# Late attention: probabilities transposed by VectorE in squares of 32 and exchanged by DMA through memory

## The chip, the cores and the metric

The kernel runs on one core of one Trainium2 chip. Its time is the time of one execution on the device, in microseconds (us), the median of several runs. Engines: TensorE (PE; its weight loads PEld), VectorE (DVE), ScalarE (ACT), GpSimd (POOL), SyncE (SP). DMA transfers are issued from the queues of SP and ACT and carried by 16 DMA engines.

## What is computed

Two transformer blocks over 256 tokens of width 1024, all in float32: a first block (convolution mixer, attention and long convolution, each with a mixture of experts) and a second one of two layers. The change lies in the mixer of the second block, cut here to what matters:

```python
for l in range(DEPTH):                                   # 2 layers
    x = x + 0.5 * swiglu(rms_norm_2(x, ffn1_norm[l]), ...)
    z = rms_norm_2(x, mix_norm[l]) @ w_in[l]
    qa, ka, va, qs, ks_, vs, zg = jnp.split(z, splits, axis=-1)
    o_na = neighbourhood_attention(qa, ka, va, na_rpb[l])      # 8 heads of 64: softmax(q k + bias) v
    o_sw = sliding_window_gqa(qs, ks_, vs, t5_bias, sw_sink[l])  # 8 heads, 2 key heads, a sink in the sum
    g = jax.nn.sigmoid(zg + b_gate[l]).reshape(B, S, N_BRANCHES, D)
    merged = g[:, :, 0] * (o_na @ w_branch_na[l]) + g[:, :, 1] * (o_sw @ w_branch_sw[l])
    x = x + merged @ w_out[l]
    x = x + 0.5 * swiglu(rms_norm_2(x, ffn2_norm[l]), ...)
```

For each head, p is the softmax over 256 keys for 256 queries (256 x 256 numbers); the product p v sums over keys, so p is needed with the keys on the partitions, while the softmax has the queries there.

## The kernel before

Each engine has a program of its own, written out in order, and waits for the others through semaphores. `sync_program` streams all weights through a ring in pieces of 1 or 2 MB, in the order of use (line 844). `tensor_program`, `scalar_program`, `vector_program` and `pool_program` each have the same stages.

The late attention is in `mixer_2` of the tensor program (from line 1774) and in `layer` of the others. It goes through eight pairs of heads, m = 0 to 7; pairs 0 to 3 are of the first kind (neighbourhood), 4 to 7 of the second (window, with a sink). With each pair one gate column (m) of `w_in` is worked off beside it, in a seven-product scheme whose weight differences POOL makes. PE's loop (from line 1903) does for pair m: `turned(m - 1)` (lines 1862 to 1870), eight transposes of 128x128, four for each head, in banks 2 and 3; `scores(m)` (line 1847) into banks 0 and 1; `values(m - 2)` (line 1872) into bank 6; `gates_first(m)` and `gates_rest(m)` into banks 4 and 5. After the loop come the last transposes and values, and `branch(p, n)` (line 1888), sixteen products each; `branch(p, 1)` needs the outputs of all eight pairs.

DVE (loop from line 3493) does `softmax(m)` (line 3449): scores plus bias with their least value, line 3459, then, when the exponentials are there, the reciprocal of the sum (3466, 3468) and the scaling (3471); then `gates(m)` (line 3473), five additions and products over banks 4 and 5. PE may overwrite these banks with `gates_first(m + 1)` when `gate_sums` of m is done.

ACT (loop from line 2473) does `turned(m - 1)` (line 2467), two copies of the transposed probabilities from banks 2 and 3 into `y.PT`, with the order of the queries in each half reversed; `values(m - 2)` (line 2471), a copy into `y.OUT2`; `softmax(m)` (2455, 2459), the exponentials with their sums; `gate_first(m)` (2440); `gates(m - 1)` (2446), the sigmoids. Exponentials and sigmoids each load their table anew.

The feed-forward of the same layers turns its hidden units in another way: DVE transposes squares of 32 (line 3277), ACT writes the result to memory (`spill`, line 2313) and reads it back in another order, in pieces of 128 bytes (`bring_back`, line 2322). The bias of the first kind is read by SP in pieces of 256 bytes, four DMAs in a row (line 823).

## Time and profile before

| what | value |
|---|---|
| time, median of 3 runs (lowest to highest) | 2544.48 us (2544.22 to 2552.77) |
| the profiled execution's own time, and its span | 2544.48 us, 2543.2 us |
| mean granted clock of PE | 0.998 of full speed |
| PE busy | 2451.7 us (96%) |
| DVE, ACT, POOL busy | 1249.2 us (49%), 437.9 us (17%), 178.7 us (7%) |
| attention of layer 0, of layer 1 (on PE) | about 1612 to 1691 us, 2206 to 2285 us |
| DMA queue of SP; of ACT | 92304 packets, 682.66 MB; 101180 packets, 28.35 MB |

The span reaches from the first to the last instruction. Busy time is the time in which an engine executes; register, semaphore and DMA-issuing instructions are not counted. In a timeline a row gives the start, the length and the engine, the line, the operation with its output and inputs, and how many instructions were merged; in brackets stands the idle time before it and what ended it. ACTq and SPq are the DMA issues of an engine's own queue; their length is the time that the trace gives the issue itself, not the transfer. The waits and the chain name what an engine waited for.

### The profile page before, as it was taken

Reading aid. Unit: us, or ns where it says so; the run is one execution under the profiler, and the core shown is the slowest. Engines: PE = TensorE matmul, PEld = TensorE weight load, DVE = VectorE, ACT = ScalarE, POOL = GpSimd, SP = SyncE. Lnnn points to the kernel's source line nnn. Section 1 sums busy time; section 2 is a strip of 40 time slices with the busy share of each in tenths; the row PEclk is TensorE's granted clock in tenths of the full one; section 3 lists DMA queues with packets and bytes.
Section 4 is the critical chain, followed back from the end, with each engine's and each line's share of the span. In section 5 each row is a group of like instructions: output and inputs, shape, how many; then the busy total and the mean of one; then the engine's idle time right before and its main releaser. Section 6 shows DMA issues by size and latency. Waiting matters only on the chain.

```text
span 2543.2 us, 29763 instructions
## 1 busy us (share of the span) xinstructions
PE 2451.7 (96%) x12358; PEld 1567.5 (62%) x12358; DVE 1249.2 (49%) x2237; ACT 437.9 (17%) x1102; POOL 178.7 (7%) x126
## 2 busy tenths in 40 slices
PE   9999999888999999987889999999999999999999
PEld 5347443424578753332348866888866875888884
DVE  4994321212176621110117666545776775654774
ACT  2111110101123210000001002641101100470110
POOL 0011000000000000000000011430001003240000
PEclk9999999999999999999999999999999999999999
DMA  9854999999984499999999863415674974423671
GB/s 395 330 233 178 371 425 426 427 428 427 423 340 166 172 376 427 426 428 428 427 422 347 255 227 149 150 67 211 212 230 153 253 231 153 173 105 138 220 223 40
DMA packets 193618, 712.90 MB, mean 280 GB/s; under 512 B 117252, under 2 KB 121860, under 8 KB 128332
## 3 DMA queue, kind: packets, MB, share of 16 engines
q1 hardware_dynamic: 92304, 682.66, 67.6%
q10 hardware_dynamic: 101180, 28.35, 5.4%
q8 instruction: 98, 1.61, 0.3%
q14 instruction: 36, 0.29, 0.0%
HBM read 698.36 MB, written 12.60 MB: 280 GB/s over the span
## 4 chain that ended last, share of the span: by engine, by line
PE 79%; DMA 16%; DVE 4%; ACT 1%; issue 0%; POOL 0%; SPq 0%; another core or an unknown queue 0%; DVEq 0%; POOLq 0%
PE bank L867 77%; DMA ring<-in_stream 8%; DMA ring_high<-in_stream 4%; DMA ring_low<-in_stream 4%; PE bank L870 2%; DVE hidden L2892 1%; DVE ab_z L2717 1%; DMA hidden_turned<-normed 1%; DVE moe_results L2917 0%; POOL ab_ln_sum L3584 0%; DVE ring L3228 0%; DVE cd_y L2524 0%; DVE moe_turned L2913 0%; ACT normed L2243 0%; ACT hidden L2243 0%
## 5 line engine op out<-in xcount | busy, mean ns | idle before, releaser
L867 PE MATMUL bank<-ring,gates 128*128 128x256 f32 (+1 forms) x1760 | 433.6, 391 | 3.1 <-DVE ring L3228 2.1
L867 PE MATMUL bank<-ring,moe_chosen 128*64 128x512 f32 (+1 forms) x2352 | 400.3, 491 | 27.7 <-DMA ring<-in_stream 27.6
L867 PEld LDWEIGHTS bank<-ring,gates 128*128 128x128 f32 x1760 | 333.6, 190 | 70.7 <-issue 22.7
L867 PE MATMUL bank<-ring,normed 128*128 128x256 f32 x1448 | 339.6, 380 | 2.0 <-ACT normed L2328 1.3
L867 PEld LDWEIGHTS bank<-ring,moe_chosen 128*64 128x64 f32 x2352 | 150.6, 137 | 246.9 <-issue 200.4
L867 PEld LDWEIGHTS bank<-ring,normed 128*128 128x128 f32 x1448 | 273.1, 190 | 41.6 <-issue 3.9
L867 PE MATMUL bank<-normed,ring 128*128 128x256 f32 (+2 forms) x1152 | 289.8, 406 | 2.3 <-DVE normed L2698 1.5
L867 PEld LDWEIGHTS bank<-normed,ring 128*128 128x128 f32 x1152 | 189.4, 190 | 99.9 <-issue 85.4
L867 PE MATMUL bank<-ring,ffn_hidden 128*128 128x512 f32 (+1 forms) x416 | 179.3, 561 | 0.0
L2917 DVE COPY moe_results<-bank 32x512 f32<-32x512 f32 x36 | 24.8, 690 | 245.2 <-PE bank L867 244.8
L2908 DVE TENSOR_TENSOR moe_silu<-bank,moe_silu 128x512 f32<-128x512 f32 x32 | 22.1, 691 | 246.8 <-PE bank L867 246.8
L3228 DVE TENSOR_TENSOR ring<-ring,ring 128x1024 f32<-128x1024 f32 x117 | 142.1, 1215 | 1.6
L867 PE MATMUL bank<-ring,moe_turned 128*64 128x512 f32 x560 | 125.2, 595 | 17.4 <-DMA ring<-in_stream 14.3
L867 PEld LDWEIGHTS bank<-ring,ffn_hidden 128*128 128x128 f32 (+1 forms) x416 | 70.8, 182 | 86.3 <-issue 76.2
L2350 ACT ACTIVATE gates<-gates,small 128x256 f32<-128x256 f32 x88 | 44.4, 507 | 412.7 <-DVE gates L3241 226.2
L2164 ACT COPY moe_results<-bank 32x512 f32<-32x512 f32 x36 | 20.7, 575 | 467.1 <-PE bank L867 466.8
L867 PEld LDWEIGHTS bank<-ring,moe_turned 128*64 128x64 f32 x560 | 40.0, 137 | 98.6 <-issue 81.7
L2717 DVE SCALAR_TENSOR_TENSOR ab_z<-ab_pad_b,vectors,ab_z 128x512 f32<-128x512 f32 x120 | 90.2, 752 | 4.3
L3228 DVE TENSOR_TENSOR ring<-ring 128x1024 f32<-128x1024 f32 x71 | 85.8, 1208 | 0.0
L867 PE MATMUL bank<-ring,hidden 128*128 128x512 f32 x168 | 84.5, 592 | 0.0
L3308 DVE TENSOR_TENSOR ring<-ring 128x512 f32<-128x512 f32 x88 | 62.1, 705 | 38.2 <-PE bank L867 38.2
L3600 POOL TENSOR_TENSOR na_bias<-na_bias,na_mask 128x512 f32<-128x512 f32 x16 | 21.4, 1370 | 782.5 <-PE bank L867 782.5
(468 smaller groups left out, 2705.4 us busy)
## 6 DMA issues: line engine op xcount, KB each, us to landing
ring<-in_stream SPq DMA_DIRECT2D x318, 1024.0 KB, 7.3
ring<-in_stream SPq DMA_DIRECT2D x117, 2048.0 KB, 30.8
ring_low<-in_stream SPq DMA_DIRECT2D x7, 2048.0 KB, 43.8
ring_far<-in_stream SPq DMA_DIRECT2D x7, 2048.0 KB, 44.6
ring_high<-in_stream SPq DMA_DIRECT2D x6, 2048.0 KB, 44.8
hidden_turned<-normed ACTq DMA_DIRECT2D x44, 256.0 KB, 7.2
ffn_hidden<-hidden_turned ACTq DMA_DIRECT2D x44, 256.0 KB, 7.4
hidden<-in_stream SPq DMA_DIRECT2D x9, 1024.0 KB, 30.9
```

The costliest lines, as they stand in the source:

```text
L867: return nc.tensor.matmul(o, lhsT, rhs, start=start, stop=stop, skip_group_check=True)
L870: return nc.tensor.transpose(o, x, ident[0:x.shape[0], 0:x.shape[0]])
L2164: ins = nc.scalar.copy(m.YG[CAP * e:CAP * e + CAP, i, 0:512], bank[4][CAP * i:CAP * i + CAP, :])
L2350: nc.scalar.activation(y.sg[:, t, :], (y.C2 if t else y.C1)[:, 0, :], ACT.Silu, scale=y.rinv_t[:, t:t + 1]).then_inc(*done.up((tag, l, "si ...
L2717: ins = v.scalar_tensor_tensor(out=z_j, in0=ab.PB[:, :, k:k + T], scalar=tap("conv_b", k, j), in1=z_j, op0=ALU.mult, op1=ALU.add)
L2892: v.scalar_tensor_tensor(out=H[:, s, n, :], in0=bank[5 + n % 3][:, T * i:T * i + T], scalar=M.MOD[:, l, 5, n, s:s + 1], in1=H[:, s, n, :], ...
L2908: v.tensor_tensor(m.SG, bank[1][:, :], m.SG, ALU.mult).then_inc(*done.up((tag, "hidden", g, e)))
L2917: ins = v.tensor_copy(m.YG[CAP * e:CAP * e + CAP, i, 512:1024], bank[4][64 + CAP * i:64 + CAP * i + CAP, :])
L3228: v.tensor_tensor(tw[:, i], a, b, ALU.subtract).then_inc(*done.up((tag, l, "t", c, i)))
L3308: v.tensor_tensor(to[:, i], a, b, ALU.subtract).then_inc(*done.up((tag, l, "dt", c, i)))
L3600: nc.gpsimd.tensor_tensor(part, part, mask, ALU.add).then_inc(*done.up(("na_bias", l, t) if h == NA_H - 2 else None))
```

## The change

For pairs 0 to 6 the transposes on PE and the copies on ACT go. The probabilities of a pair lie in one tensor `y.SC` of 128x1024, ordered so that squares of 32x32 follow each other (`probs_of`; pair 7 keeps the plain order). DVE transposes all squares at once into `y.turned`. ACT writes that to memory with four DMAs (`spill_probs`, 32 partitions each, rows of 512 bytes), and one pair later reads it back with two DMAs in pieces of 128 bytes (`bring_probs`) into `y.pairs`, which holds the keys on the partitions. The values of a pair are computed three pairs later (`LAG`) in place of two, from there; pair 7 is still transposed by PE and copied by ACT. The reversal of the queries is now in ACT's copy of the values. DVE's order changes: a gate column's sums and scaling are split into `gates_first`, `gates_summed` and `gates_scaled`, the latter two placed in the next pair around `biased`. Behind the loop, PE does values(5), two branches, values(6), values(7), then the other branches; values(7) has bank 7.

The diff, without the new semaphores and the two buffers in memory:

```diff
--- before.py
+++ after.py
@@ -614,9 +614,9 @@
     y.keys_by_token = y.C1[:, :, 0:P]
     y.sq8, y.sq8_heads = M.H[:, 1], heads[:, 0:KB * T].rearrange("p (n t) -> p n t", t=T)
     y.hid, y.hid_turned = spare[:, 0:512], ctx_u[:, 0:512]
-    y.SC = [spare[:, 512 * n:512 * n + 512].rearrange("p (t k) -> p t k", t=TT) for n in range(2)]
-    y.PT = [[x[:, 512 * n:512 * n + 512].rearrange("p (k q) -> p k q", k=TT) for n in range(2)]
-            for x in (spare[:, 1024:2048], M.ring[WEIGHT_SUMS[0]][:, SLOT:SLOT + 1024])]
+    y.SC, y.turned = spare[:, 0:1024], spare[:, 1024:2048]
+    y.pairs = [M.ring[WEIGHT_SUMS[0]][:, SLOT + 1024 * n:SLOT + 1024 * n + 1024] for n in range(2)]
+    y.PT = [[x.rearrange("p (k i q) -> p i k q", k=TT, i=2)[:, i] for i in range(2)] for x in y.pairs]
     y.t1 = [y.KA[:, 2 * n:2 * n + 2, :] for n in range(2)]
     y.g8, y.stats = [M.small[:, 2 * l:2 * l + 2] for l in range(LAYERS)], M.small[:, 16:16 + 16 * 8]
     y.rinv_t, y.rinv_8 = M.small[:, 144:144 + TT], M.small[:, 146:146 + TT]
@@ -696,6 +696,16 @@
 def wide(x, n):
 
     return x.rearrange("p (o t) -> p o t", o=1).broadcast_to([P, n, x.shape[1]])
+
+
+def probs_of(y, m, i, t):
+
+    order = "i t k f" if m == NA_H - 1 else "k i t f"
+    return y.SC.rearrange(f"p ({order}) -> p i t k f", i=2, t=TT, f=32)[:, i, t]
+
+
+def by_pieces(x):
+    return x.rearrange("p (k f) -> p k f", f=32)
 
 
 def reversed_queries(x):
@@ -853,6 +865,8 @@
 
 
 VALUES_BANK = (4, 5)
+VALUES_AT = (6,) * (NA_H - 1) + (7,)
+LAG = 3
 KEYS_BANK = 6
 
 
@@ -1862,11 +1876,9 @@
         def turned(m):
             for i in range(2):
                 pe.wait_ge(*V.at(("probs_2", l, m, i)))
-                if m:
-                    pe.wait_ge(*A.at(("turned_2", l, m - 1, i)))
                 for k in range(TT):
                     for t in range(TT):
-                        ins = turn(bank[2 + i][:, T * k + P * t:T * k + P * t + P], y.SC[i][:, t, P * k:P * k + P])
+                        ins = turn(bank[2 + i][:, T * k + P * t:T * k + P * t + P], flat(probs_of(y, m, i, t)[:, 4 * k:4 * k + 4]))
                 ins.then_inc(*done.up(("turned_2", l, m, i)))
 
         def values(m):
@@ -1877,12 +1889,11 @@
                 pe.wait_ge(*V.at(("head_normed", l, "ks")))
             if kind:
                 pe.wait_ge(*V.at(("vs", l)))
-            for i in range(2):
-                pe.wait_ge(*A.at(("turned_2", l, m, i)))
+            pe.wait_ge(*(A.at(("turned_2", l, m, 1)) if m == NA_H - 1 else S.probs_in.at((l, m))))
             for k in range(TT):
                 for i, (h, p0) in enumerate(heads):
                     v = y.VS[:, k, DH * (h // 4):DH * (h // 4) + DH] if kind else y.VA[:, k, DH * h:DH * h + DH]
-                    ins = mm(bank[6][p0:p0 + DH, 0:T], v, y.PT[m % 2][i][:, k, :], k == 0, k == TT - 1)
+                    ins = mm(bank[VALUES_AT[m]][p0:p0 + DH, 0:T], v, y.PT[m % 2][i][:, k, :], k == 0, k == TT - 1)
             ins.then_inc(*done.up(("values_2", l, m)))
 
         def branch(p, n):
@@ -1893,6 +1904,8 @@
             pe.wait_ge(*A.at(("out_2", l, NA_H // 2 * (n + 1) - 1)))
             if p >= 2:
                 pe.wait_ge(*V.at(("gated", l, p - 2, n)))
+            elif p:
+                pe.wait_ge(*A.at(("turned_2", l, NA_H - 1, n)))
             for half in range(2):
                 for k in range(4):
                     ins = mm(bank[b][:, T * half:T * half + T], ring.tile(name)[:, k, 256 * off + P * half:256 * off + P * half + P],
@@ -1902,20 +1915,19 @@
 
         pairs = NA_H
         for m in range(pairs):
-            if m:
-                turned(m - 1)
             scores(m)
-            if m >= 2:
-                values(m - 2)
+            if m >= LAG:
+                values(m - LAG)
             gates_first(m)
             gates_rest(m)
             if m == 1:
                 keys_turned()
         turned(pairs - 1)
+        values(pairs - 3)
+        branch(0, 0)
+        branch(1, 0)
         values(pairs - 2)
-        branch(0, 0)
         values(pairs - 1)
-        branch(1, 0)
         branch(0, 1)
         branch(1, 1)
         for p in range(2, KB // 2):
@@ -2456,34 +2468,57 @@
                                          bias=M.sinks[:, l, h:h + 1]).then_inc(*done.up())
                 for t in range(TT):
                     n = 2 * i + t
-                    nc.scalar.activation(y.SC[i][:, t, :], y.SC[i][:, t, :], ACT.Exp, bias=st[:, n:n + 1], scale=-1.0,
+                    nc.scalar.activation(probs_of(y, m, i, t), probs_of(y, m, i, t), ACT.Exp, bias=st[:, n:n + 1], scale=-1.0,
                                          accum_out=st[:, 4 + n:5 + n]).then_inc(*done.up(("exp_2", l, m, i, t)))
+
+        def spill_probs(m):
+
+            act.wait_ge(*V.at(("turned_2", l, m)))
+            if m >= 2:
+                act.wait_ge(*S.probs_in.at((l, m - 2)))
+            for a in range(4):
+                rows = bass.AP(tensor=probs_blocks[m % 2].tensor, offset=a * 32 * 1024, ap=[[128, 32], [32 * 128, 8], [1, 128]])
+                nc.scalar.dma_start(rows, y.turned[32 * a:32 * a + 32, :].rearrange("p (k n) -> p k n", k=8)).then_inc(
+                    *S.probs_out.up((l, m) if a == 3 else None))
+
+        def bring_probs(m):
+
+            act.wait_ge(*S.probs_out.at((l, m)))
+            if m >= 2:
+                act.wait_ge(*TE.at(("values_2", l, m - 2)))
+            for k in range(TT):
+                rows = probs_blocks[m % 2].rearrange("(a k p x f) -> k p x a f", a=4, k=TT, p=P, f=32)[k]
+                to = y.pairs[m % 2].rearrange("p (k x a f) -> p k x a f", k=TT, a=4, f=32)[:, k]
+                nc.scalar.dma_start(to, rows).then_inc(*S.probs_in.up((l, m) if k == TT - 1 else None))
 
         def turned(m):
             for i in range(2):
                 act.wait_ge(*TE.at(("turned_2", l, m, i)))
-                if m >= 2:
-                    act.wait_ge(*TE.at(("values_2", l, m - 2)))
-                nc.scalar.copy(reversed_queries(flat(y.PT[m % 2][i])), bank[2 + i][:, :].rearrange("p (n q) -> p n q", q=P)).then_inc(*done.up(("turned_2", l, m, i)))
+                act.wait_ge(*TE.at(("values_2", l, m - 2)))
+                nc.scalar.copy(y.PT[m % 2][i], bank[2 + i][:, :].rearrange("p (k q) -> p k q", k=TT)).then_inc(*done.up(("turned_2", l, m, i)))
 
         def values(m):
             act.wait_ge(*TE.at(("values_2", l, m)))
-            nc.scalar.copy(y.OUT2[:, m, :], bank[6][:, 0:T]).then_inc(*done.up(("out_2", l, m)))
+            nc.scalar.copy(reversed_queries(y.OUT2[:, m, :]), bank[VALUES_AT[m]][:, 0:T].rearrange("p (n q) -> p n q", q=P)).then_inc(*done.up(("out_2", l, m)))
 
         for m in range(NA_H):
             if m:
-                turned(m - 1)
+                spill_probs(m - 1)
             if m >= 2:
-                values(m - 2)
+                bring_probs(m - 2)
             softmax(m)
+            if m >= LAG:
+                values(m - LAG)
             gate_first(m)
             if m:
                 gates(m - 1)
             if m == 1:
                 keys_out()
+        values(NA_H - 3)
         turned(NA_H - 1)
+        bring_probs(NA_H - 2)
+        gates(NA_H - 1)
         values(NA_H - 2)
-        gates(NA_H - 1)
         values(NA_H - 1)
         squares("ffn2", y.sq8_heads, lambda p: V.at(("hidden", l, "mix", p)))
         ffn(2)
@@ -2496,6 +2531,7 @@
 
     distances = nc.dram_tensor("distance_bias", (SW_H, 2 * T), F32, kind="Internal").ap()
     turned_blocks = [nc.dram_tensor(f"hidden_turned{i}", (P * 2 * T,), F32, kind="Internal").ap() for i in range(2)]
+    probs_blocks = [nc.dram_tensor(f"probs_turned{i}", (P * 4 * T,), F32, kind="Internal").ap() for i in range(2)]
     mixer_ab()
     moe(0, "ab")
     mixer_cd()
@@ -3446,19 +3482,22 @@
             v.tensor_copy(y.KSX[0:DH, :], y.KS[DH:P, :]).then_inc(*done.up())
             v.tensor_copy(y.KSX[DH:P, :], y.KS[0:DH, :]).then_inc(*done.up(("ks_swapped", l)))
 
-        def softmax(m):
+        def biased(m):
             kind, blk = divmod(m, NA_H // 2)
             st = y.stats[:, 64 * (m % 2):64 * (m % 2) + 64]
             dve.wait_ge(*TE.at(("scores_2", l, m)))
             dve.wait_ge(*(I["sw_bias"].at(TT - 1) if kind else S.pool.at(("na_bias", l, TT - 1))))
             for i in range(2):
                 h, top = 2 * blk + i, st[:, 2 * i:2 * i + 2]
-                if m:
-                    dve.wait_ge(*TE.at(("turned_2", l, m - 1, i)))
                 for t in range(TT):
-                    v.tensor_tensor_reduce(out=y.SC[i][:, t, :], in0=bank[i][:, T * t:T * t + T], in1=(y.SW_BIAS if kind else y.NA_BIAS)[:, h, t, :],
+                    v.tensor_tensor_reduce(out=probs_of(y, m, i, t), in0=by_pieces(bank[i][:, T * t:T * t + T]),
+                                           in1=by_pieces((y.SW_BIAS if kind else y.NA_BIAS)[:, h, t, :]),
                                            scale=-1.0, scalar=y.minus_sinks[:, h:h + 1] if kind else -3.0 * NEG, op0=ALU.add, op1=ALU.min,
                                            accum_out=top[:, t:t + 1]).then_inc(*done.up(("biased", l, m, i) if t else None))
+
+        def probs(m):
+            kind = m // (NA_H // 2)
+            st = y.stats[:, 64 * (m % 2):64 * (m % 2) + 64]
             for i in range(2):
                 total, extra = st[:, 4 + 2 * i:6 + 2 * i], st[:, 8 + 2 * i:10 + 2 * i]
                 dve.wait_ge(*A.at(("exp_2", l, m, i, TT - 1)))
@@ -3468,22 +3507,36 @@
                 v.reciprocal(total, total).then_inc(*done.up())
                 dve.wait_ge(*done.now())
                 for t in range(TT):
-                    v.tensor_scalar(y.SC[i][:, t, :], y.SC[i][:, t, :], total[:, t:t + 1], None, ALU.mult).then_inc(*done.up(("probs_2", l, m, i) if t else None))
-
-        def gates(c):
-
+                    part = probs_of(y, m, i, t)
+                    v.tensor_scalar(part, part, total[:, t:t + 1], None, ALU.mult).then_inc(*done.up(("probs_2", l, m, i) if t else None))
+
+        def turned(m):
+            dve.wait_ge(*done.at(("probs_2", l, m, 1)))
+            if m:
+                dve.wait_ge(*S.probs_out.at((l, m - 1)))
+            v.transpose(y.turned, y.SC).then_inc(*done.up(("turned_2", l, m)))
+
+        def gate_parts(c):
             b, d = (bank[x][:, :].rearrange("p (n t) -> p n t", t=P) for x in VALUES_BANK)
-            to = y.gates_of[c].rearrange("p (n t) -> p n t", t=P)
+            return b, d, y.gates_of[c].rearrange("p (n t) -> p n t", t=P)
+
+        def gates_first(c):
+            b, d, to = gate_parts(c)
             dve.wait_ge(*A.at(("gate_first", l, c)))
-            v.tensor_tensor(to[:, 0:4:3, :], b[:, 1:3, :], wide(to[:, 3, :], 2), ALU.add).then_inc(*done.up())
+            v.tensor_tensor(to[:, 0:4:3, :], b[:, 1:3, :], wide(to[:, 3, :], 2), ALU.add).then_inc(*done.up(("gate_firsts", l, c)))
+
+        def gates_summed(c):
+            b, d, to = gate_parts(c)
             dve.wait_ge(*S.chunk.at(("in_2", l, 9 + c)))
-            dve.wait_ge(*done.now())
+            dve.wait_ge(*done.at(("gate_firsts", l, c)))
             v.tensor_tensor(to[:, 1:3, :], d[:, 0:2, :], wide(to[:, 3, :], 2), ALU.add).then_inc(*done.up())
             dve.wait_ge(*done.now())
             v.tensor_tensor(to[:, 3, :], to[:, 1, :], d[:, 1, :], ALU.add).then_inc(*done.up())
             dve.wait_ge(*done.now())
             v.tensor_tensor(to[:, 1:3, :], to[:, 1:3, :], d[:, 2:4, :], ALU.add).then_inc(*done.up(("gate_sums", l, c)))
-            dve.wait_ge(*done.now())
+
+        def gates_scaled(c):
+            dve.wait_ge(*done.at(("gate_sums", l, c)))
             by_block = y.gates_of[c].rearrange("p (n t) -> p n t", t=T)
             v.tensor_tensor(by_block, by_block, wide(y.rinv, 2), ALU.mult).then_inc(*done.up(("gate", l, c)))
 
@@ -3491,12 +3544,21 @@
         dve.wait_ge(*done.now())
         dve.wait_ge(*S.chunk.at(("in_2", l, 8)))
         for m in range(NA_H):
-            softmax(m)
+            if m:
+                gates_summed(m - 1)
+            biased(m)
+            if m:
+                gates_scaled(m - 1)
+            probs(m)
+            if m < NA_H - 1:
+                turned(m)
+            gates_first(m)
             if m == 0:
                 keys_scaled()
             if m == 2:
                 keys_swapped()
-            gates(m)
+        gates_summed(NA_H - 1)
+        gates_scaled(NA_H - 1)
         dve.wait_ge(*A.at(("gate", l, KB - 1)))
         for p in range(KB // 2):
             for n in range(2):
```

## Rows read from the trace of the kernel before

**Rows 1.** Stretches: length, busy PE, PEld, DVE, ACT, POOL, clock, DMA share, GB/s.

```profile
1652.00:1662.00 10.00, 10.00 (x88) 8.92 (x87) 5.75 (x21) 8.12 (x21) 5.94 (x5) 1.00 0.31 107
...
2246.00:2256.00 10.00, 10.00 (x88) 8.93 (x87) 5.75 (x21) 8.12 (x21) 5.80 (x5) 1.00 0.33 107
```

**Rows 2.** Chain of waits, 1600 to 1700 us, shares by line.

```profile
by line: PE bank L867 92.1%; PE bank L870 8.1%
```

**Rows 3.** Timeline of PE, one pair: start, us, line, operation, tiles, shape.

```profile
1656.47 1.04 PE L870 MATMUL bank<-kept,hidden 128*128 128x128 f32 x8
...
1657.43 1.13 PE L867 MATMUL bank<-ffn_hidden 64*128 64x256 f32 x8
...
1658.50 1.08 PE L867 MATMUL bank<-ring,ffn_hidden 128*64 128x256 f32 x8
...
1659.51 2.05 PE L867 MATMUL bank<-normed,ring 128*128 128x128 f32 x16
...
1664.97 1.06 PE L867 MATMUL bank<-normed,ring 128*128 128x128 f32 x8
...
1665.87 1.04 PE L870 MATMUL bank<-kept,hidden 128*128 128x128 f32 x8
```

**Rows 4.** One line's instructions, DVE's transpose: ns min/median/max, first and last start.

```profile
L3277 DVE STREAM_TRANSPOSE normed<-hidden x44: 711/711/712, 1366.2 to 2473.1; 128x512 f32<-128x512 f32 x44
```

**Rows 5.** Timeline of DVE, the same pair, after the last exponential.

```profile
1663.79 0.16 DVE L3466 TENSOR_TENSOR small<-small 128x2 f32<-128x2 f32 x1 [0.16 <-ACT hidden L2459]
...
1664.19 0.61 DVE L3471 TENSOR_SCALAR hidden<-hidden,small 128x256 f32<-128x256 f32 x2
```

**Rows 6.** Timeline of ACT, the same pair.

```profile
1660.02 1.28 ACT L2455 ACT_TABLE_LOAD   x1
...
1663.67 0.24 ACT L2440 COPY gates<-bank 128x128 f32<-128x128 f32 x1
...
1666.50 1.08 ACT L2467 COPY ring<-bank 128x512 f32<-128x512 f32 x2 [0.37 <-PE bank L870]
```

**Rows 7.** DMA issues of three lines: ns of the issue, min/median/max.

```profile
L2313 ACTq DMA_DIRECT2D hidden_turned<-normed x44: 326/4628/16291, 1366.9 to 2473.9; - x44
...
L2322 ACTq DMA_DIRECT2D ffn_hidden<-hidden_turned x44: 587/587/4127, 1374.3 to 2485.2; - x44
...
L823 SPq DMA_DIRECT2D na_bias<-in_na_rpb x32: 601/636/1218, 1372.3 to 2009.0; - x32
```

**Rows 8.** Timeline of ACT (ACTq: its DMA issues), two places in the feed-forward.

```profile
1455.27 0.59 ACTq L2322 DMA_DIRECT2D ffn_hidden<-hidden_turned  x1
...
1457.08 0.60 ACTq L2313 DMA_DIRECT2D hidden_turned<-normed  x1
...
1770.54 0.37 ACT L2328 COPY normed<-bank 128x256 f32<-128x256 f32 x1 [0.49 <-PE bank L867]
...
1770.54 0.61 ACTq L2322 DMA_DIRECT2D ffn_hidden<-hidden_turned  x1
...
1771.40 4.71 ACTq L2313 DMA_DIRECT2D hidden_turned<-normed  x1
...
1776.64 0.51 ACT L2350 ACTIVATE gates<-gates,small 128x256 f32<-128x256 f32 x1 [5.74 <-DVE gates L3241]
```

**Rows 9.** DMA: one load's landing, 1656 to 1664; queues, 1770.5 to 1774 (packets, MB, share).

```profile
ring<-in_stream SPq DMA_DIRECT2D x1, 1024.0 KB, 4.9
...
q1 hardware_dynamic: 179, 1.34, 96.1%
```

**Rows 10.** Timeline of ACT and PE, end of the last pair.

```profile
1682.38 0.19 ACT L2459 ACTIVATION_READ_ACCUMULATOR hidden<-hidden,small 128x1 f32 x1
...
1685.63 1.08 PE L867 MATMUL bank<-hidden,ffn_hidden 128*64 128x256 f32 x8
...
1686.65 3.72 PE L867 MATMUL bank<-normed,ring 128*128 128x256 f32 x16
...
1686.76 0.37 ACT L2471 COPY normed<-bank 128x256 f32<-128x256 f32 x1 [0.39 <-PE bank L867]
```

More of the change, by code:

```diff
@@ L725, in signals @@
     S.hidden = Signal(nc, "in_hidden", known, 16)
+    S.probs_out = Signal(nc, "out_probs", known, 16)
+    S.probs_in = Signal(nc, "in_probs", known, 16)
     S.sent = Signal(nc, "out_sent", known, 16)
@@ L3613, in program @@
     pool_program(nc, a, M, S, ring)
-    every = [S.tensor, S.scalar, S.vector, S.pool, S.chunk, S.distance, S.spilled, S.hidden, S.sent, *S.landed, *S.into.values()]
+    every = [S.tensor, S.scalar, S.vector, S.pool, S.chunk, S.distance, S.spilled, S.hidden, S.probs_out, S.probs_in, S.sent, *S.landed, *S.into.values()]
     return {x.name: x.table for x in every}
```

## The prediction

> **What bounds the kernel now.** I read three views in this order. The table by stretches shows the stage that changes: in ten microseconds of late attention TensorE (PE) is busy for all ten at full clock, ScalarE (ACT) for 8.12, VectorE (DVE) for 5.75, and the DMA engines for a third of the time; layer 1 looks the same [rows 1]. The chain of waits over layer 0's attention is PE alone, 8.1% of it transposes [rows 2]. So PE's work is the time here, and a microsecond taken from it is one gained, as long as ACT, DVE and the transfers keep up. PE's timeline gives the slots of one pair, from start to start: transposes 1656.47 to 1657.43, 0.96; scores 1.07; values 1.01; gates 5.46, then 0.90 more. The next transposes start at 1665.87, a period of 9.40 [rows 3].
>
> The profiled execution took 2544.48 us, of which the span is 2543.2; it is also the median of the three runs shown, so the sum is made against 2544.5.
>
> **Taken from PE.** Transposes of seven pairs in each of two layers leave: 14 x 0.96 = 13.4 us [rows 3]. That is the ceiling of the gain. The period could fall to 8.44. The reversed order of queries moves from one copy to another of the same kind: nothing.
>
> **Put on DVE.** One transpose of 128x1024 a pair. The trace has 128x512 at 0.71 [rows 4]; between that and twice it, 1.42, I take 1.3, since it has twice the elements. DVE was busy for 5.75 of 10 [rows 1], 5.4 a pair, and with 1.3 still has room under 8.44. What counts is its place: spill_probs waits for it. From the last exponential, DVE's row of sums starts at 1663.79 and the scaled rows end at 1664.80 [rows 5]; with the transpose and its hand-overs that is 2.4 us from exponential to first spill (2.2 for the first kind, which has no sink).
>
> **Put on ACT: six DMA issues a pair.** This decides. Two copies go (1.08 [rows 6]); four spills and two brings come, in ACT's own order. Behind them wait the exponentials of the next pair, behind those DVE's scaling and gates_first, and behind those PE's gates of the pair after. A DMA issue holds what follows on its queue: the spill of the feed-forward takes 0.33 at least, 4.63 in the median, 16.3 at most; its bring, of 128-byte pieces as here, 0.59 in the median [rows 7]. The timeline says why: a spill issued 0.25 after a bring took 4.71, one issued 1.2 after a bring in a quiet stretch 0.60 [rows 8]. The second issue is held while the first transfer's pieces are not yet drained. The change has two brings of 2048 pieces each, one right behind the other, with four spills ahead of them.
>
> Call B the time from the first spill to the end of the second bring.
> - Low end: every issue at its lowest row, 4 x 0.33 + 2 x 0.59, with five gaps of 0.04: 2.7 us.
> - Issues back to back, nothing held: the loads of na_bias, four in a row on SP, have 0.64 each [rows 7]. 0.33 + 3 x 0.68 + 2 x 0.63 = 3.6 us.
> - High end: the second bring held as the feed-forward's spill is, from 1770.54 to 1776.11 = 5.6 [rows 8]: 0.33 + 3 x 0.68 + 5.6 = 8.0 us.
> - I take 4.8. With nothing else on the queues the spills' pieces should be gone some 3.5 us after the first issue, and then the second bring is taken: 4.1 (an estimate, from the 0.60 in the quiet stretch). On top, a weight load of 1 MB lands 4.9 us after its issue, and in the 3.5 us after the bring at 1770.54 only the weight queue moved, 179 packets and none of ACT's [rows 9]. One load falls into each pair, and I let it cost 0.7 on average. Between ends of 2.7 and 8.0 this lies nearest to the unheld case, because the attention's DMA share is a third, not full.
>
> The Trainium skill, page DMA: Bandwidth & Descriptors, section Queues, rings and completion order, says that each DMA engine takes turns between the queues; the 179 packets disagree. By its rule the 0.7 would be nothing and the sum 8 us lower.
>
> **The sum.** From one pair's last exponential to the next: 2.4 to the transpose's end, B, then 3.75 from ACT's table load at 1660.02 to the end of the last exponential, 0.1 after the copy's start at 1663.67 [rows 6]. So 6.15 + B for the second kind, 5.55 + B for the first. ACT's other work (values, gate copy, table load and sigmoids) lies beside DVE's 2.4, and a DMA can be issued while a copy still runs (bring and copy begin together at 1770.54 [rows 8]). With B = 4.8 a pair takes 10.95 or 10.35 in place of 9.40: ACT sets the pace, not PE. Spills run from pair 1, brings from pair 2:
> - pair 1: one lot of spills ahead of its exponentials, partly beside DVE's work: +0.5
> - pairs 2 and 3: 2 x 0.95 = +1.9
> - pairs 4 to 7: 4 x 1.55 = +6.2
> - end: before, the last exponential ended at 1682.57 and the last transposes' slot at 1685.63 [rows 10], 3.06 later, since PE was at the gates. A PE that waits has done those and needs 1.6: -1.5
> - new order behind it: values(7) stands right ahead of branch(0, 1), which needs ACT's copy of it; before, a branch of 3.7 us lay between. Copy 0.37 and two hand-overs: +0.65. values(6) waits for the last two brings, which ACT issues after its copies of the last pair; two branches, 7.4 us, cover them: nothing. Without that cover it would be what is left of a bring's landing, up to those 7.4 [rows 10].
>
> That is 7.8 a layer, 15.6 in both: 2544.5 + 15.6 = **2560 us**. One microsecond of B is 12 us of the time (six pairs, two layers). Values three pairs behind hide the landings: a bring has the rest of its pair, some 5 us, and the values behind it another; PE has slack of two microseconds by then.
>
> **Rivals.**
> - Issues aren't held. B is 2.7 to 3.6; then the first kind's pair takes 8.44 to 9.15 and the second's 8.85 to 9.75, and the time is 2536 to 2546: not slower. One mechanism, deciding from B = 3.3, where the second kind's period is again 9.40. For it: the one quiet row, 0.60. Against it: 2048 pieces stood alone ahead of that one. The Trainium skill, same page, section Issuing engines are not separate DMA queues, calls the time to initiate a DMA usually small beside the DMA; by that this rival would be the likely one, and the 4.71 of the rows speaks against it.
> - The second bring is held as the feed-forward's spill is, in each pair: B = 8.0, 54 us more, 2598. For it: the median of 4.63. Against it: where those issues are held, weights pass without a break, 1.34 MB in 3.5 us [rows 9]; the attention has 1 MB in a whole pair.
> - ACT's DMA issues run wholly beside its arithmetic, and PE stays the bound: 13.4 less twice 0.65, 2532. Against it: the activation after the 4.71 us issue began only when that was over (1776.64 [rows 8]).
>
> **How the numbers follow.** Forecast, 2552 to 2571: 0.50. Issues not held, 2536 to 2551: 0.25. Held throughout, 2572 to 2600: 0.20. PE the bound, 2532: 0.05. The range 2536 to 2590 leaves out the last and the upper half of the third. About 0.5% (12.7 us) is what a measurement of this kernel can tell from no change. Faster by more needs nearly the whole ceiling: 0.03. Slower by more, above 2557: all of the held case and three quarters of the forecast, 0.57. The rest, 0.40, is within.
>
> **What would show it.** In the profile after: ACT's DMA rows of the second bring near 1.5 us and up; the pair's period on PE near 10.9 in the second half, with idle time of PE that ends on DVE's gate sums; and no PE work for seven of eight transposes. A period of 8.4 and PE at ten in ten would show me wrong, and so would a second bring at 0.6.

## The result, and the profile after

The changed kernel takes 2588.24 us (median of six runs, 2587.23 to 2589.01) against 2544.26 for the kernel before beside it: 1.0168 times, with an interval of 1.0155 to 1.0182. The forecast was 2560, with a range of 2536 to 2590: slower, as forecast, and inside the range, but by 44 us in place of 16.

The page after: PE is busy for 95% of a longer span, though it has less to do; ACT's DMA queue carries 14.7 MB more.

```profile
span 2587.7 us, 29613 instructions
...
PE 2456.8 (95%) x12246; PEld 1571.3 (61%) x12246; DVE 1280.6 (49%) x2251; ACT 421.5 (16%) x1074; POOL 179.1 (7%) x126
...
q10 hardware_dynamic: 174204, 43.03, 8.2%
```

The table by stretches over the attention of layer 0 (length; busy PE, PEld, DVE, ACT, POOL; granted clock; DMA share; GB/s) answers [rows 1]. PE was busy for ten of ten there. Now it has gaps in every stretch, and from the second on its granted clock is a mean of 0.80 to 0.87, so for part of the time the lower of its two levels (1.2 and 2.4 GHz), which also makes its busy time longer.

```profile
1613.80:1641.00 27.20, 23.99 (x203) 21.91 (x202) 16.00 (x53) 12.22 (x37) 13.50 (x11) 1.00 0.63 181
1641.00:1667.00 26.00, 20.99 (x146) 18.38 (x147) 17.23 (x47) 13.91 (x38) 8.84 (x7) 0.80 0.68 157
1667.00:1692.00 25.00, 19.39 (x146) 17.23 (x144) 15.44 (x41) 11.15 (x27) 9.74 (x8) 0.86 0.69 170
1692.00:1718.00 26.00, 20.98 (x128) 17.41 (x129) 11.40 (x36) 12.96 (x33) 0.44 (x1) 0.87 0.56 140
```

One pair on ACT's timeline, from the last exponential of pair 3 to that of pair 4 (start, us, line; L2471 exponentials, L2481 spills, L2492 brings, L2467 the sink's exponential):

```profile
1653.13 0.18 ACT L2471 ACTIVATION_READ_ACCUMULATOR hidden<-hidden,small 128x1 f32 x1
...
1655.47 1.34 ACTq L2481 DMA_DIRECT2D probs_turned<-hidden  x3
...
1656.85 0.50 ACTq L2481 DMA_DIRECT2D probs_turned<-hidden  x1
1657.38 5.32 ACTq L2492 DMA_DIRECT2D ring<-probs_turned  x2
1662.73 1.28 ACT L2467 ACT_TABLE_LOAD   x1 [5.46 <-issue]
...
1666.29 0.19 ACT L2471 ACTIVATION_READ_ACCUMULATOR hidden<-hidden,small 128x1 f32 x1
```

The three parts of the forecast's sum can be read off. From 1653.31, the end of the exponentials, 2.16 to the first spill; B, from 1655.47 to the end of the second bring at 1662.70, is 7.23; 3.78 more to the end of the next exponentials. Between bring and exponentials ACT does nothing: 5.46 us of idle time, put down to its own issues. Together 13.2, where before a pair took 9.40 [rows 3]. All pairs of the two layers, read in the same way (the parts of a pair add up to its time):

| us | pair 2 | 3 | 4 | 5 | 6 | 7 |
|---|---|---|---|---|---|---|
| layer 0: exponentials to first spill | 4.09 | 3.43 | 2.16 | 5.08 | 2.36 | 2.36 |
| B | 8.23 | 4.22 | 7.23 | 4.68 | 6.88 | 3.96 |
| end of bring to end of exponentials | 3.40 | 3.40 | 3.78 | 3.77 | 3.77 | 3.77 |
| layer 1: exponentials to first spill | 4.18 | 4.60 | 2.16 | 5.94 | 2.36 | 2.36 |
| B | 7.23 | 3.88 | 7.52 | 3.85 | 6.95 | 4.36 |

ACT's waits over layer 0's attention (1612 to 1722 us: total, times, longest) point the same way. They put the idle time ahead of the exponentials down to the landing of ACT's own spills or to its issues; the exponentials themselves wait for no landing, and the rows above show the issues back to back, with gaps of 0.04 at most, so that the length of the issues is what holds them.

```profile
ACT L2467 <- DMA probs_turned<-hidden: 17.5, 3, 7.2
...
ACT L2471 <- DMA probs_turned<-hidden: 7.8, 1, 7.8
ACT L2467 <- issue: 5.5, 1, 5.5
```

From pair 0 to pair 7 the exponentials now take 84.2 us in layer 0 and 84.9 in layer 1, against 65.2 before: 38.6 us of the 44.5 by which the span grew. The ends of the two layers, from pair 7's exponentials to `branch(0, 1)`, account for 2.5 and 1.4 more, and 1.6 lie ahead of the attention, in stages that the change doesn't touch. (Layer 0's first scores start at 1612.24 before and 1613.82 after; over the ten profiled executions of this document they start between 1609.92 and 1613.82.)

### The profile page after: what moved, and what is told of

The parts are those of the page before. It is cut to its first block, busy times and chain, and to the rows that moved or that the text cites. A ratio compares the mean times of both kernels' runs of the same rounds, so it can differ in the third digit from the quotient of the medians.

```text
span 2587.7 us, 29613 instructions
## 1 busy us (share of the span) xinstructions
PE 2456.8 (95%) x12246; PEld 1571.3 (61%) x12246; DVE 1280.6 (49%) x2251; ACT 421.5 (16%) x1074; POOL 179.1 (7%) x126
## 4 chain that ended last, share of the span: by engine, by line
PE 74%; DMA 16%; DVE 5%; ACT 2%; ACTq 1%; issue 1%; POOL 0%; another core or an unknown queue 0%; DVEq 0%; POOLq 0%
PE bank L881 73%; DMA ring<-in_stream 7%; DMA ring_high<-in_stream 4%; DMA ring_low<-in_stream 4%; PE bank L884 2%; ACTq L2492 1%; DVE hidden L2928 1%; DVE ab_z L2753 1%; DMA hidden_turned<-normed 1%; ACT hidden L2471 1%; DMA probs_turned<-hidden 1%; DVE hidden L3511 0%; DVE hidden L3517 0%; ACT L2467 0%; ACTq L2481 0%
## 5 line engine op out<-in xcount | busy, mean ns | idle before, releaser
L881 PE MATMUL bank<-normed,ring 128*128 128x256 f32 (+2 forms) x1152 | 301.3, 420 | 31.1 <-DVE gates L3536 16.9
L881 PEld LDWEIGHTS bank<-normed,ring 128*128 128x128 f32 x1152 | 199.6, 202 | 130.5 <-issue 116.4
L881 PE MATMUL bank<-ring,ffn_hidden 128*128 128x512 f32 (+1 forms) x480 | 188.9, 543 | 9.6 <-ACT ring L2458 5.3
```

Source lines behind the costliest of these rows:

```text
L881: return nc.tensor.matmul(o, lhsT, rhs, start=start, stop=stop, skip_group_check=True)
```

## The experiments

The theory from the trace: the six DMA issues on ACT's queue stand in front of the exponentials and set the pace (B), and PE waits. Rivals: VectorE's new order, or the longer way through memory itself, is what costs. What B consists of is a second question, and what else made the loss so large a third. Each kernel ran beside the kernel before, which had 2544.3 (first four) and 2544.6 (last four) there.

**The issues moved from ACT to SP**, to the place where SP waits for pair m's gate column to come free; the same DMAs, ahead of that column's load; each bring also waits until the one before has landed.

```diff
         for m in range(NA_H):
-            if m:
-                spill_probs(m - 1)
-            if m >= 2:
-                bring_probs(m - 2)
             softmax(m)
...
         for i, n in transfers(ring.plan):
+            if ring.to_be_free(i, n) in after_chunk:
+                l, m = after_chunk[ring.to_be_free(i, n)]
+                if m < NA_H - 1:
+                    spill_probs(l, m)
+                if m:
+                    bring_probs(l, m - 1)
             if ring.to_be_free(i, n):
                 sp.wait_ge(S.chunk.sem, ring.to_be_free(i, n))
```

> The changed kernel with its spills and brings issued by SP, at the point where SP would wait for the pair's gate column to be free, and with each bring waiting for the landing of the one before it. Theory H (ACT is held by its DMA issues, 5.8 us a pair from the first spill to the end of the second bring, and that sets the pair's period): ACT's list falls to 6.5 us, PE's slots of 8.44 set the pace again in most pairs, 2532 to 2548 us. Rival O (the new order of DVE's work, DVE's longer list and the values three pairs behind cost the time, the issues little): 2575 to 2590 us. Rival P (transfers land too late for the values, wherever they are issued): idle time of PE ahead of the values, 2560 or more.

Measured: 2544.62 (2542.34 to 2550.44), 1.0004 times before (0.9995 to 1.0014). All of the 44 us are gone while the same bytes go the same way through memory, and VectorE has the same work and order. In the late pairs PE is without a gap and its period is 8.53, the 8.44 of the forecast's ceiling within 0.1. On PE's timeline (no row has an idle time before it), scores, values, and gates follow each other at 1657.77 and 1666.30:

```profile
1657.77 1.13 PE L916 MATMUL bank<-ffn_hidden 64*128 64x256 f32 x8
1658.83 1.08 PE L916 MATMUL bank<-ring,ffn_hidden 128*64 128x256 f32 x8
1659.85 2.05 PE L916 MATMUL bank<-normed,ring 128*128 128x128 f32 x16
1661.74 3.74 PE L916 MATMUL bank<-gates,ring 128*128 128x128 f32 x32
1665.31 1.06 PE L916 MATMUL bank<-normed,ring 128*128 128x128 f32 x8
1666.30 1.14 PE L916 MATMUL bank<-ffn_hidden 64*128 64x256 f32 x8
```

So the place of the issues is the cause. But nothing of the 13.4 us was gained: PE's waits in the attention of layer 0 (below) were 3.6 us for VectorE's gate sums, in pairs 1 and 3, and 1.0 for ACT's copies of values in the end. The granted clock was 0.92 from 1634 to 1655: behind the second of those waits 48 matmuls of the gates took 3.41 and 4.02 in place of 2.05 and 3.74, 1.6 more.

```profile
PE bank L916 <- DVE ring L3545: 3.6, 2, 2.2
PE bank L916 <- ACT normed L2517: 1.0, 2, 0.6
```

**The brings in pieces of 2048 bytes**, 128 to a DMA in place of 2048 of 128 bytes, which puts what `values` reads in another order.

```diff
-                rows = probs_blocks[m % 2].rearrange("(a k p x f) -> k p x a f", a=4, k=TT, p=P, f=32)[k]
-                to = y.pairs[m % 2].rearrange("p (k x a f) -> p k x a f", k=TT, a=4, f=32)[:, k]
+                rows = probs_blocks[m % 2].rearrange("(p k n) -> k p n", k=TT, p=P)[k]
+                to = y.pairs[m % 2].rearrange("p (k n) -> p k n", k=TT)[:, k]
```

> The changed kernel with brings that read as many bytes in pieces of 2048 bytes (128 in each DMA in place of 2048); the probabilities come in the wrong order, so the attention's values are not those of the reference. Theory H, with the hold set by the number of pieces not yet drained: the second bring is issued in about 0.6 us, first spill to end of second bring 3 to 3.6 us in every pair in place of 4 to 8, about 2.4 us less in each of twelve pairs: 2553 to 2563 us. Were the hold set by bytes, or by the weight loads alone: 2580 to 2590. Rival O: 2585 to 2590.

Measured: 2553.68 (2552.64 to 2561.70), 1.0042 times before (1.0028 to 1.0057). B is 3.72 in the mean of the twelve pairs, a little above the 3 to 3.6 that were expected. The brings' issues (ns, min/median/max), in the changed kernel and then in this one:

```profile
L2492 ACTq DMA_DIRECT2D ring<-probs_turned x28: 587/968/5203, 1633.0 to 2323.4; - x28
```

```profile
L2492 ACTq DMA_DIRECT2D ring<-probs_turned x28: 326/530/1591, 1632.3 to 2288.7; - x28
```

The hold on the second bring is that of the many small pieces: with the same bytes in few pieces it is all but gone. Even so the kernel is slower than before, since the four spills and two brings still stand in the pair's chain.

**The second bring behind the exponentials.**

```diff
                 spill_probs(m - 1)
             if m >= 2:
-                bring_probs(m - 2)
+                bring_probs(m - 2, (0,))
             softmax(m)
+            if m >= 2:
+                bring_probs(m - 2, (1,))
```

> The changed kernel with ACT's second bring moved behind the exponentials, some 4 us after the first. Theory H: the second bring finds the first drained and takes 0.6, so that 2.5 us lie ahead of the exponentials and 0.6 behind: a pair of about 9.1 to 9.8 us, 2545 to 2560 us in all. Rival O: 2585 to 2590 us.

Measured: 2553.95 (2551.66 to 2556.72), 1.0039 times before (1.0025 to 1.0054). 34 us come back by moving one issue of six. Part of the hold remains, now in front of the gate's copy: in pair 2 the second bring takes 4.23 us, the exponentials that were already on the engine run beside it, and the copy waits for 2.21.

```profile
1634.44 4.23 ACTq L2492 DMA_DIRECT2D ring<-probs_turned  x1
...
1636.31 0.19 ACT L2471 ACTIVATION_READ_ACCUMULATOR hidden<-hidden,small 128x1 f32 x1
1638.71 0.27 ACT L2452 COPY ring<-bank 128x128 f32<-128x128 f32 x1 [2.21 <-issue]
```

**VectorE's new order alone**, in the kernel before (PE's transposes and ACT's copies kept, no exchange).

```diff
         for m in range(NA_H):
-            softmax(m)
+            if m:
+                gates_summed(m - 1)
+            biased(m)
+            if m:
+                gates_scaled(m - 1)
+            probs(m)
+            gates_first(m)
...
-            gates(m)
```

> The kernel before with only DVE's new order (a gate column's sums and scaling placed around the next pair's bias), transposes on PE and values two pairs behind as they were. Theory H: PE stays the bound, the same time as before within 3 us, 2541 to 2548. Rival O: a part of the loss shows here, 2555 us or more.

Measured: 2544.90 (2542.17 to 2546.66), 1.0001 times before (0.9991 to 1.0010). The new order costs nothing by itself, so this rival falls.

**Small weight loads during the attention.**

```diff
+            if ring.to_be_free(i, n) in late_chunks:
+                to, src = to[:, 0:128], src[:, 0:128]
             nc.sync.dma_start(to, src).then_inc(*ring.arrival(i).up(i if last else None))
```

> The changed kernel with the weight loads that SP issues as the gate columns of late attention come free (8 a layer) cut to 64 KB of their 1 MB; what they should have brought are weights of later stages, so the output is not the reference's. B, from ScalarE's first spill to the end of its second bring, is 8.2, 4.2, 7.2, 4.7, 6.9, 4.0 in pairs 2 to 7 of layer 0 of the changed kernel. Theory: the long ones have a load's packets ahead of ScalarE's on the engines. Without them B is 4.0 to 4.5 in every pair, 12 x 1.4 = 17 us less: 2571 (2565 to 2575). Rival 1 (the second bring is held by its own queue's pieces alone, and alternates with something of the attention's own order): B keeps its two values, 2588 within 3. Rival 2 (all of the hold is the loads'): B falls to 3.0 to 3.6, 2558 to 2563.

Measured: 2564.26 (2562.30 to 2566.71), 1.0080 times before (1.0065 to 1.0095) and 24.0 below the changed kernel. B is 4.82, 4.25, 4.99, 3.94, 3.85, 5.51 in layer 0 and 3.84 to 4.52 in layer 1: 4.33 in the mean, in place of 5.75. The brings' issues here:

```profile
L2500 ACTq DMA_DIRECT2D ring<-probs_turned x28: 587/954/2980, 1629.1 to 2297.8; - x28
```

So B is about 4.3 by itself, and 1.4 on average, some 3 in every second pair, is the weight load that SP has just issued; both rivals fall. The trace of the changed kernel shows the load at work. In layer 0 the loads are issued at 1630.4, 1657.5 and 1682.1, within 2 us of the first spills of pairs 2, 4 and 6, and at 1638.3, 1666.0 and 1690.6, by the end of these pairs' brings or behind it; none is issued during B in pairs 3, 5 and 7. From 1659.5 to 1661.5, while pair 4's second bring is held, the weight queue moved 92 packets (0.75 MB) and ACT's queue 4; pairs 2 and 6 have such a stretch too (80 packets against 1 from 1632.2 to 1634.2, 94 against none from 1683.8 to 1686.2). The time fell by 7 us more than 12 x 1.42 = 17: see the price of B below.

**GpSimd's weight differences left out.**

```diff
-                nc.gpsimd.tensor_tensor(gt[:, i], *terms[i], ALU.subtract).then_inc(*done.up(("gate_t", l, c, i)))
...
-            gate_product(d[:, P:2 * P], y.GT[c % 2][:, 0], y.US[:, 0])
+            gate_product(d[:, P:2 * P], tile[:, 0:4, P:2 * P], y.US[:, 0])
```

> The changed kernel (2588.2 us) without GpSimd's weight differences in late attention: the gate products of PE take the raw weight tile in the place of the differences, so the gates are not those of the reference; PE's count of matmuls is the same. In the trace of the changed kernel, VectorE takes 2.2 to 2.4 us from the last exponential to the end of its transpose, but 3.4 after pair 2 and 5.1 after pair 4 of layer 0, where GpSimd works on its differences in the same microseconds (scaling of two blocks 2.14 and 2.51 us in place of 0.61). Theory: GpSimd's work slows VectorE's on the path. Then these two stretches fall to 2.2 to 2.4, 1.1 + 2.7 us a layer, and the time to about 2580 (2577 to 2583). Rival: VectorE is slowed by the transfers that read its tile, or by the banks: then the two stretches stay long, and the time is 2588 within 2.

Measured: 2575.77 (2573.76 to 2578.74), 1.0124 times before (1.0111 to 1.0138) and 12.5 below the changed kernel, somewhat more than expected. B is unchanged, 5.70 in the mean. The stretches from the exponentials to the first spill that were 3.43 and 5.08 in layer 0, 4.60 and 5.94 in layer 1, are 2.16, 2.35, 2.16 and 2.36: 19.05 has become 9.03, 10.0 us. That of pair 2 is 4.09 in both layers. In the changed kernel, DVE's rows after pair 4's exponentials stand against GpSimd's (POOL) like this:

```profile
1666.10 1.38 POOL L3634 TENSOR_TENSOR ring<-ring 128x512 f32<-128x512 f32 x1 [3.01 <-PE bank L881]
1667.55 1.27 POOL L3634 TENSOR_TENSOR ring<-ring,ring 128x512 f32<-128x512 f32 x1
1668.78 1.31 POOL L3634 TENSOR_TENSOR ring<-ring 128x512 f32<-128x512 f32 x1
1670.05 1.31 POOL L3634 TENSOR_TENSOR ring<-ring,ring 128x512 f32<-128x512 f32 x1
```

```profile
1666.50 0.99 DVE L3505 TENSOR_TENSOR small<-small 128x2 f32<-128x2 f32 x1 [0.16 <-ACT hidden L2471]
...
1667.73 2.51 DVE L3511 TENSOR_SCALAR hidden<-hidden,small 128x256 f32<-128x256 f32 x2
1670.27 1.25 DVE L3517 STREAM_TRANSPOSE hidden<-hidden 128x1024 f32<-128x1024 f32 x1
```

and without GpSimd's work:

```profile
1664.03 0.62 DVE L3508 TENSOR_SCALAR hidden<-hidden,small 128x256 f32<-128x256 f32 x2
1664.68 1.25 DVE L3514 STREAM_TRANSPOSE hidden<-hidden 128x1024 f32<-128x1024 f32 x1
```

A sum of two numbers a partition takes 0.99 in place of the 0.16 of [rows 5] and ends at 1667.49, where GpSimd's first difference ends (1667.48); two scalings take 2.51 in place of 0.62. The transpose, which runs beside the last of the four, is not slowed. Nor are VectorE's rows that read a bank: the bias of pair 4 (line 3493) takes 0.48 for each 128x256 from 1658.58 to 1660.20, beside GpSimd's differences, and 0.48 from 1696.87, where GpSimd is idle; the gate's product behind it, between tiles, takes 1.77 in place of 0.69.

```profile
1658.58 0.48 DVE L3493 CUSTOM_DVE_ANT_0 hidden<-bank,sw_bias,small 128x256 f32<-128x256 f32 x1
...
1660.20 1.77 DVE L3541 TENSOR_TENSOR ring<-ring,late_rinv 128x512 f32<-128x512 f32 x1
```

**Eight transposes a pair back on PE, unread**, ahead of the scores of pairs 1 to 7.

```diff
+        def turned_unread():
+            for i in range(2):
+                for k in range(4):
+                    turn(bank[2 + i][:, P * k:P * k + P], U[:, 0, k, 0:P])
         for m in range(pairs):
+            if m:
+                turned_unread()
             scores(m)
```

> The changed kernel with the eight transposes a pair put back on PE ahead of the scores of pairs 1 to 7, on other data, into the free banks 2 and 3, and read by nobody: 14 x 0.96 = 13.4 us more of PE's work. Theory (ScalarE's queue sets the pace of the pair, PE waits): the 13.4 us fall into PE's waits, and the time stays at 2588 within 2; it falls to 2583 to 2586 if, with shorter idle time, PE's granted clock in the attention (0.80 to 0.87 in the changed kernel) comes back towards 1.0 and the last transposes end nearer to the last exponential than 3.6 us. Rival (PE is still the bound of most pairs): 2588 + 13 = 2601, or what part of it lies on the path.

Measured: 2580.85 (2578.94 to 2582.66), 1.0143 times before (1.0129 to 1.0157). With 13.4 us more of work for PE the kernel is 7.4 us faster than the changed one, more than the 2 to 5 us that were expected at best. The rival, that PE still bounds most pairs, falls. The granted clock over the attention (the same columns as above) is higher, and 1.00 in the end:

```profile
1638.00:1663.00 25.00, 18.88 (x144) 17.10 (x143) 16.50 (x44) 11.99 (x30) 9.03 (x7) 0.86 0.67 165
1663.00:1688.00 25.00, 21.83 (x174) 19.43 (x173) 16.33 (x45) 12.86 (x34) 10.05 (x8) 0.93 0.67 169
1688.00:1713.00 25.00, 21.50 (x144) 17.16 (x145) 10.58 (x33) 12.08 (x30) 2.10 (x1) 1.00 0.61 148
```

The last transposes now end 1.75 after pair 7's exponentials in both layers, where the changed kernel has 3.67 and 2.59. That is 2.8 of the 7.4; most of the rest is a shorter B in pair 6 (5.47 and 5.58 for 6.88 and 6.95).

**SP's issues, the keys' work moved, and another end.** From the first experiment's kernel (the waits that follow from PE's and ACT's new order change with it):

```diff
             biased(m)
             if m:
                 gates_scaled(m - 1)
+            if m == 1:
+                keys_scaled()
+            if m == 3:
+                keys_swapped()
             probs(m)
...
-            if m == 0:
-                keys_scaled()
-            if m == 2:
-                keys_swapped()
...
         branch(0, 0)
-        branch(1, 0)
-        values(pairs - 2)
         values(pairs - 1)
+        values(pairs - 2)
+        branch(1, 0)
         branch(0, 1)
```

> The kernel whose spills and brings SP issues (2544.6 us), with two more edits: VectorE works on the keys (their scaling and their swap) while ScalarE makes the exponentials of pairs 1 and 3, and not behind pairs 0 and 2; and behind the loop PE does values(5), branch(0,0), values(7), values(6), branch(1,0), branch(0,1), so that a branch covers each copy of values. Theory: the losses left there were PE's waits for VectorE's gate sums in pairs 1 and 3 (1.44 and 2.21 us, and 1.6 for the low clock after the second) and 1.03 in the end of a layer. Without them 2544.6 - 2 x 5.7 = 2533 (2531 to 2537), close to before less the 13.4 us of transposes. Rival: the waits move on (VectorE's gate sums stay late for another reason, or values(6) waits for its bring's landing): 2541 to 2545.

Measured: 2537.08 (2532.58 to 2538.68), 0.9969 times before (0.9956 to 0.9981): faster than the kernel before, by 7.5 us (0.3%, clear of 1 by its interval), and than the changed one. PE's waits over layer 0's attention are down to these (layer 1 has 1.0 for the gate sums and 1.7 for the brings):

```profile
PE bank L916 <- DVE ring L3546: 1.0, 2, 0.7
PE bank L916 <- DMA ring<-probs_turned: 0.7, 1, 0.7
```

From layer 0's first scores to the start of `branch(0, 1)` it is 78.5 us (1613.82 to 1692.28, the latter from the start of `branch(1, 0)` at 1688.63 and 3.65 for a branch), against 82.7 before (1612.24 to 1694.96): 4.3 of the 6.7 that a layer's transposes cost. The 2532 of the forecast's third rival, PE as the bound, is thus some 5 us away once another engine issues the DMAs and these waits of PE are shortened; the rival's mechanism, issues that run beside ACT's arithmetic, is not what got there. The time lies at the upper edge of what was expected; the waits above are part of what is left.

## Why the prediction came out as it did

**What bounds the kernel before, and the ceiling.** Right: with nothing in ACT's way the pair takes 8.53 on PE.

**The mechanism.** Right: ACT's issues stand ahead of the exponentials, ACT sets the pace, PE waits, and the time rises. Moving the issues takes away all of it, and PE's extra work fits into its waits. The signs that the forecast named are there: a second bring from 1.33 to 5.20 us, PE waiting for VectorE's gate sums, and a pair of 10.1 to 13.6 in the second half (forecast 10.95).

**The size: the step that failed.** The forecast's sum was 15.6, the difference measured 44. What failed is the price of three terms. VectorE's stretch from exponentials to spill was taken as undisturbed in every pair, with ACT's other work beside it at nothing and GpSimd's not thought of: 2 x (2 x 2.2 + 4 x 2.4) = 28.0 in the sum, 41.1 measured. A weight load was to cost B 0.7 on average: it cost 1.4. And the end of a layer was to be 0.85 shorter: it was 2.5 and 1.4 longer. The result lies in the stretch that the forecast gave 0.20 (held throughout, 2572 to 2600), not in its own (2552 to 2571, given 0.50), and the range held it only because it reached into that rival. Term by term:

- B, "I take 4.8": the mean is 5.75, 0.95 x 12 = 11.4 us. The 4.1 of the forecast without loads was near the 4.33 measured without them. What failed is the 0.7 for the weight load: it takes 1.4 on average, since in every second pair the load stands ahead of nearly the whole bring (B of 6.9 to 8.2, where the forecast's high end was 8.0) and in the others it doesn't (3.9 to 4.7). The forecast took the two ends for rival cases; they alternate.
- VectorE's 2.4 from exponential to spill: twelve stretches sum to 41.1 in place of 28.0, 13.1 us, more than B. Where nothing disturbs them they are 2.16 and 2.36, as forecast, and the transpose is 1.25 for 1.3. But in pairs 3 and 5 GpSimd works at the same time: 9.8 us of the 13.1. The trace before has this too (scalings of 0.35 in the median, the longest 1.355), beside a PE that was the bound, and the forecast didn't look for it. And for pair 2, "ACT's other work lies beside DVE's 2.4" was wrong: sigmoids and the keys' copy, which waits for PE, come ahead of the spill, 1.9 and 2.0 us; without GpSimd it is still 4.09 there.
- The end, -1.5 + 0.65: from pair 7's exponentials to `branch(0, 1)` 14.93 and 13.84 were measured, 12.40 before and 11.55 by the forecast, 5.7 us off in both layers. PE was to stand ready and need 1.6; it needed 3.6 in layer 0, because it had waited for the gate sums and then ran at a low clock. PE's timeline at this place, changed kernel, shows 16 matmuls of 3.76 behind that wait where [rows 3] have 2.05, and two waits of 0.47 and 0.56 for the copies of values. Only one of these had been counted, and the third values that a lag of three leaves behind the loop (1.0) not at all.

```profile
1697.10 3.76 PE L881 MATMUL bank<-normed,ring 128*128 128x128 f32 x16 [2.69 <-DVE gates L3536]
...
1705.74 1.04 PE L884 MATMUL bank<-kept,hidden 128*128 128x128 f32 x8
1706.71 1.08 PE L881 MATMUL bank<-ring,ffn_hidden 128*64 128x256 f32 x8
...
1716.38 1.08 PE L881 MATMUL bank<-ring,ffn_hidden 128*64 128x256 f32 x8 [0.47 <-ACT normed L2502]
1718.03 2.18 PE L881 MATMUL bank<-normed,ring 128*128 128x256 f32 x9 [0.56 <-ACT normed L2502]
```

- The other way go pairs 2 and 4, which took 10.49 and 9.77 before and not 9.40 (-2.9), and pair 1 (-0.5). 11.4 + 13.1 + 5.7 - 3.4 = 26.8; with 15.6 that is 42.4 of 44, and 1.6 lie ahead of the attention.

**The landings.** "Values three pairs behind hide the landings" failed once a layer. PE's row of values(0), in pair 3 of layer 0, has 5.34 us of idle time before it. The waits put it down to a sigmoid of ACT that ends at that moment, but `values` has no wait for a sigmoid; it waits for the second bring of pair 0, which was issued at about 1633.7 and landed after 10.9 us (the longest landing of that line), at 1644.6, as the row begins. In layer 1 the wait at this place is 1.08 and put down to the bring. The wait of layer 0 lies beside ACT's own chain, but the 16 matmuls behind it took 3.75 in place of 2.05.

```profile
1644.66 1.98 PE L881 MATMUL bank<-ring,ffn_hidden 128*64 128x256 f32 x8 [5.34 <-ACT ring L2458]
1647.98 3.75 PE L881 MATMUL bank<-normed,ring 128*128 128x128 f32 x16 [1.35 <-DVE ring L3536]
```

**The price of B.** "One microsecond of B is 12 us" was too low between these kernels: from 5.75 to 4.33 (small loads) the time fell by 24.0, from there to 3.72 (long pieces) by 10.6, 17 us for one. The profiled executions show what the rest is. Between those of the changed kernel and of the small loads, 25.7 us apart, B gives 17.0, VectorE's stretches from exponentials to spill 2.4, and the ends of the layers 2.8 (13.0 in both, from 14.93 and 13.84); 3.4 lie ahead of the first attention, where the edit changes nothing. From the small loads to the long pieces, 8.8 us apart, B gives 7.4 and VectorE's stretches 4.9, and the part ahead of the attention takes 2.8 back. So B itself costs its 12, and the rest is VectorE's stretches, the ends, and scatter ahead of the attention; why the stretches and the ends shrink with B no run separates.

**The rivals.** "Issues aren't held" fell: the median of 0.97 over all 28 brings hides that the first of each two takes 0.6 and the second up to 5.2. The Trainium skill, page DMA: Bandwidth & Descriptors, section Issuing engines are not separate DMA queues, calls the time to initiate a DMA usually small beside the DMA; here the second bring's was 1.3 to 5.2 against landings of 5.5 in the median, and the loss was gone when SP had the issues. "Held in each pair" came nearest in its number, 2598, but a B near its 8.0 comes in every second pair only; that the time came so near is in part luck, since VectorE's stretches and the ends make up much of it.

## What to carry to other kernels

Here a DMA issue cost its engine up to 5.2 us while the pieces ahead of it drained: put an exchange of many small pieces on a queue behind which no work of the path stands, and count the loads of other queues in the same stretch as part of its price. When a step moves onto another engine, look also at which engine beside it will then run in the same microseconds, and price the whole stretch with rows that ran beside that engine's work, not with the median. PE, which was the bound and now waits, got slower at its own work, too: 16 matmuls of 3.76 in place of 2.05.

## What the runs showed of the hardware

- Some of VectorE's instructions are held while GpSimd works, all of them between tiles in SBUF, the core's on-chip memory: 0.99 us for a sum of two numbers a partition (0.16 alone), ending with GpSimd's instruction within 0.01; 2.51 for two scalings (0.62 alone); 1.77 for the gate's product of 128x512 (0.69 in the pairs beside it). VectorE's transpose of squares, 1.25, and its bias rows, which read a bank (0.48 with and without), were not held beside GpSimd. The Trainium skill, page SBUF — State Buffer, section SBUF: two separate sides, describes an exclusive lock on a port pair that VectorE and GpSimd share, held for a whole instruction; these rows agree.
- A load of 1 MB passed nearly as a block: 92 of its packets and 4 of ACT's in the 2 us from 1659.5, while ACT's second bring was held.
- VectorE's transpose of squares of 32 takes 1.25 for 128x1024, against 0.71 for 128x512 [rows 4].
- PE's granted clock was a mean of 0.80 to 0.87 over three stretches of layer 0's attention (PE busy for 20.99 of 26.00, 19.39 of 25.00 and 20.98 of 26.00 us), where the kernel before had 1.00 and PE without a gap. With eight unread transposes a pair it was 0.86, 0.93 and, in the end of layer 0, 1.00.
- Instructions that stood ahead of a DMA issue on ACT run on beside it (exponentials during the 4.23 us issue above); what stands behind it doesn't start.
